# Attention logits of token tiles 4 to 7: two heads at a time in two column parts, with four logit buffers in place of two

## The chip, the cores and the metric

The kernel runs on one core of a Trainium2 chip. The metric is the device time of one execution in microseconds (us). Three runs of the kernel before gave 2792.24, 2794.49 and 2781.63 us, so the median is 2792.24 us.

The engines are PE (TensorE, matmuls), PEld (its weight loads, which overlap PE), DVE (VectorE), ACT (ScalarE), POOL (GpSimd) and SP (SyncE, which only issues DMAs here). Each engine runs its own instructions in order and waits for the others at semaphores.

## The reference

Two layers of a hybrid decoder over 1024 tokens of width 1024, all in float32. A layer projects the normed input once and gives it to three groups of heads (an mLSTM, a sparse attention, a Mamba-2 scan), joins their outputs by one projection, and ends with a SwiGLU feed-forward block. The change touches the sparse attention of four heads, each 64 wide:

```
score = where(causal, score, -inf)          # of a small indexer, shared by the heads
_, sel = lax.top_k(score, top_k)            # top_k = 256
logits = q . k_sel * (d ** -0.5)            # per head
p = softmax(logits)                         # over the selected keys that are causal
out = p @ v_sel
```

The kernel gathers nothing. It computes the logits of a query with all causal keys, adds a mask (0 for a selected key, a large negative number for another) and takes the softmax over the whole row. A tile of 128 queries number c (0 to 7) has 128(c+1) keys.

## The kernel before

Per layer there is a stage A (norm, the input projection in 30 units of 128 columns, the indexer, the choice of keys, the attention), a stage B (the scans, the output projection) and a stage E (feed-forward). A barrier over all engines stands between A and B of a layer. The E of layer 0 and the A of layer 1 share a block.

**A unit of the projection** is 48 matmuls over 512 columns (each weight and each activation is kept as a high and a low part, and three of the four products are taken), issued by `eighth(u, e)` in eighths of six, L891 to L901.

**The attention** is cut into 32 steps, step m = 4c + h for tile c and head h (`divmod(m, AH)`). A step goes through five places:

- PE, `two_logits(m)` (L1045 to L1051) for tiles 0 to 3, and `logits(m)` (L1030 to L1041) for tiles 4 to 7: the dot products of 128 queries with the tile's keys, over a contraction of 64. A head's 64 rows lie in the lower or the upper half of the partitions. `two_logits` issues both heads of a pair one behind the other at every even step, head i into its own PSUM bank (bank 2 or 3), over at most 512 columns. `logits` issues one head at every step, over 640 to 1024 columns, as one matmul of 512 columns and one of the rest, into banks 2 and 3 together (`pair23`).
- DVE, `maximum(m)` (L1278 to L1290): adds the mask, writes the sum into the logit buffer `lg[m % 2]` and reduces the row's maximum (L1286), then makes the bias of the exponential out of it (L1290).
- ACT, `exps(m)` (L742 to L747): the exponential in place, with its row sum.
- PE, `turn_weights(m)` (L1054 to L1060): c+1 transposes of 128x128 into banks 4 and 5, and ACT, `turned_out(m)` (L751 to L755), which copies them to `pt[m % 2]`.
- PE, `values(m)` (L1063 to L1071): c+1 matmuls with the values, 64 columns each.

DVE divides by the row sums in `rows_out(c)` (L1297, L1299), and PE turns the result in `cat_turn(c)` (L1078).

**The order on PE** is written out by hand. `attend(k)` (L1081) issues `values(k - 4)`, `turn_weights(k - 2)`, the logits of step k, and at every fourth k a `cat_turn`. Steps 0 to 7 stand in units 22 to 25, while DVE still searches for the selection threshold bit by bit. Steps 8 to 31 stand one behind each eighth of units 27, 28 and 29, and four calls behind the last unit empty the pipeline. I call one eighth with one `attend` a slot. DVE has `choose(c + 1, part)` (L1359 to L1371) behind each `attend` of tile c: it makes the mask of the next tile in four parts, of which part 1 is a scan (L1365). ACT has the evictions of the projection (L673) and `kept_hi` (L767) between its steps.

**The waits around the logits.** `logits(m)` waits for all maxima before m, since both heads share the two banks. `maximum(m)` waits for the transposes of step m - 2, which read the same buffer. `turn_weights(m)` waits for the exponential of m and for ACT's copy of step m - 1.

## Time and profile before

| what | value |
|---|---|
| median of 3 runs | 2792.24 us (2781.63 to 2794.49) |
| span of the profiled execution | 2787.1 us |
| PE busy | 2675.3 us, 96% of the span |
| PE weight loads busy | 2157.4 us, 77% |
| DVE busy | 1822.3 us, 65% |
| ACT busy | 1114.8 us, 40% |
| POOL busy | 1233.7 us, 44% |
| mean granted clock of TensorE, as a share of full speed | 0.981 |

The page gives the profiled execution by its span, from the first to the last instruction, and no time of its own beside it. The span is 5.1 us under the median of the runs. Busy PE is not PE at its peak, because matmuls overlap in the pipeline. What an instruction costs there is therefore read from start to start: the start of a group is taken from the start of the group behind it.

### The profile page before, as it was taken

Reading aid. Unit: us, or ns where it says so; the run is one execution under the profiler, and the core shown is the slowest. Engines: PE = TensorE matmul, PEld = TensorE weight load, DVE = VectorE, ACT = ScalarE, POOL = GpSimd, SP = SyncE. Lnnn points to the kernel's source line nnn. Section 1 sums busy time; section 2 is a strip of 40 time slices with the busy share of each in tenths; the row PEclk is TensorE's granted clock in tenths of the full one; section 3 lists DMA queues with packets and bytes.
Section 4 is the critical chain, followed back from the end, with each engine's and each line's share of the span. In section 5 each row is a group of like instructions: output and inputs, shape, how many; then the busy total and the mean of one; then the engine's idle time right before and its main releaser. Section 6 shows DMA issues by size and latency. Waiting matters only on the chain. (4 is left out here: it accounts for less than half of the span.)

```text
span 2787.1 us, 36014 instructions
## 1 busy us (share of the span) xinstructions
PE 2675.3 (96%) x12868; PEld 2157.4 (77%) x12868; DVE 1822.3 (65%) x2888; ACT 1114.8 (40%) x2094; POOL 1233.7 (44%) x774
## 2 busy tenths in 40 slices
PE   7999999999899999999989999999998999999997
PEld 5677877778688888888766788777786888888886
DVE  4469865584765666665654798646748566666666
ACT  4336434574532223232433364446745222323223
POOL 1228510340665545665433284104317544566545
PEclk9999999999999999999999999999999999999999
DMA  4102320433111111111421123105221211111113
GB/s 136 46 23 77 121 69 25 139 95 120 40 53 61 61 45 45 60 45 60 130 98 28 31 83 122 62 16 168 90 105 38 68 54 46 45 60 45 63 57 129
DMA packets 186882, 199.30 MB, mean 72 GB/s; under 512 B 19313, under 2 KB 162801, under 8 KB 186497
## 3 DMA queue, kind: packets, MB, share of 16 engines
q1 hardware_dynamic: 180992, 176.63, 20.3%
q10 hardware_dynamic: 5760, 20.97, 2.0%
q8 instruction: 78, 1.28, 0.2%
q14 instruction: 52, 0.42, 0.0%
HBM read 158.78 MB, written 38.80 MB: 71 GB/s over the span
## 5 line engine op out<-in xcount | busy, mean ns | idle before, releaser
L2271 POOL TENSOR_TENSOR ring_lo<-ring_sum,ring_hi 128x512 fp32r<-128x512 f32 x200 | 306.3, 1547 | 474.7 <-ACT ring_hi L2359 474.7
L2493 PE MATMUL ps<-form_hi,ring_hi 128*128 128x512 f32 x1232 | 484.2, 393 | 23.2 <-POOL ring_lo L1524 20.2
L2493 PE MATMUL ps<-form_lo,ring_hi 128*128 128x512 f32 x1232 | 482.5, 392 | 0.0
L2493 PE MATMUL ps<-form_hi,ring_lo 128*128 128x512 f32 x1232 | 482.3, 391 | 0.0
L901 PE MATMUL ps<-act_hi,whi 128*128 128x512 f32 x960 | 395.0, 411 | 9.2 <-ACT smr L441 8.4
L901 PE MATMUL ps<-act_lo,whi 128*128 128x512 f32 x960 | 379.0, 395 | 0.0
L901 PE MATMUL ps<-act_hi,wlo 128*128 128x512 f32 x960 | 378.7, 395 | 0.0
L2359 ACT ACTIVATE ring_hi<-ring_sum 128x512 fp32r<-128x512 f32 x200 | 125.2, 632 | 627.3 <-DVE ring_sum L2569 627.1
L2581 DVE TENSOR_TENSOR yacc<-yacc,ps 128x1024 f32<-128x1024 f32 x176 | 214.8, 1220 | 243.6 <-PE ps L2519 243.6
L1328 DVE TENSOR_SCALAR_CACHE_REDUCE ties<-score,kth 128x384 uint8<-128x384 f32 (+5 forms) x396 | 348.4, 942 | 4.8
L604 POOL TENSOR_TENSOR wlo<-raw,whi 128x1024 fp32r<-128x1024 f32 x56 | 137.2, 2449 | 394.0 <-ACT whi L646 394.0
L2493 PEld LDWEIGHTS ps<-form_hi,ring_hi 128*128 128x128 f32 x1232 | 233.5, 190 | 76.2 <-POOL ring_lo L1524 14.1
L2519 PE MATMUL ps<-ring_hi,hhi 128*128 128x512 f32 x704 | 275.3, 391 | 1.1 <-POOL hlo L2282 0.6
L2519 PE MATMUL ps<-ring_lo,hhi 128*128 128x512 f32 x704 | 274.4, 390 | 0.0
L2519 PE MATMUL ps<-ring_hi,hlo 128*128 128x512 f32 x704 | 274.3, 390 | 0.0
L2493 PEld LDWEIGHTS ps<-form_hi,ring_lo 128*128 128x128 f32 x1232 | 233.2, 189 | 48.8
L2493 PEld LDWEIGHTS ps<-form_lo,ring_hi 128*128 128x128 f32 x1232 | 233.4, 189 | 48.1
L901 PEld LDWEIGHTS ps<-act_hi,whi 128*128 128x128 f32 x960 | 183.0, 191 | 77.4 <-issue 35.9
L1570 DVE TENSOR_TENSOR gate_t<-gate_t,ps 128x512 f32<-128x512 f32 x176 | 116.9, 685 | 168.4 <-PE ps L2493 168.4
L901 PEld LDWEIGHTS ps<-act_hi,wlo 128*128 128x128 f32 x960 | 183.0, 191 | 40.2
L2569 DVE TENSOR_TENSOR ring_sum<-ff_raw 128x512 f32<-128x512 f32 x200 | 209.2, 1071 | 3.2 <-DMA ff_raw<-in_w_gate 3.2
L901 PEld LDWEIGHTS ps<-act_lo,whi 128*128 128x128 f32 x960 | 183.3, 191 | 36.1 <-issue 1.9
(321 smaller groups left out, 4686.9 us busy)
## 6 DMA issues: line engine op xcount, KB each, us to landing
raw<-in_w_in SPq DMA_DIRECT2D x56, 512.0 KB, 3.8
ff_raw<-in_w_gate SPq DMA_DIRECT2D x22, 1024.0 KB, 5.3
ff_raw<-in_w_up SPq DMA_DIRECT2D x22, 1024.0 KB, 5.3
ff_raw<-in_w_down SPq DMA_DIRECT2D x22, 1024.0 KB, 5.0
proj_scratch<-stage ACTq DMA_DIRECT2D x40, 512.0 KB, 2.7
wc<-proj_scratch SPq DMA_DIRECT2D x14, 1280.0 KB, 6.6
xmid_scratch<-xres SPq DMA_DIRECT2D x16, 512.0 KB, 2.6
resid<-xmid_scratch SPq DMA_DIRECT2D x16, 512.0 KB, 6.7
```

Of the source, the lines that this page charges most:

```text
L604: pool.tensor_tensor(wlo[u % 2][:, :], raw[u % 2][:, :], whi[u % 2][:, :].bitcast(F32), ALU.subtract)\
L901: mm = pe.matmul(ps[:, half, :], w[:, k], a[half][:, k, :], start=(k == 0 and m == 0), stop=(k == KT - 1 and m == 2))
L1328: v.tensor_scalar(tie(c), of(c), at(kth, c), 0.0, op, ALU.add, accum_out=at(held, c))
L1570: v.tensor_tensor(q, q, src, op).then_inc(m_drain.sem, 1)
L2271: pool.tensor_tensor(flat_form(ring_lo[slot]), src, flat_form(ring_hi[slot]).bitcast(F32), ALU.subtract)\
L2359: act.activation(flat_form(ring_hi[slot]), src, ACT.Copy).then_inc(f_hi.sem, 1)
L2493: mm = pe.matmul(ps[:, product_bank(r, i), :], w[:, k], a[:, k], start=(k == 0 and m == 0), stop=(k == 3 and m == 2))
L2519: mm = pe.matmul(place(t)[:, cols], h[:, j, rows], w, start=(j == 0 and m == 0), stop=(j == 1 and m == 2))
L2569: v.tensor_tensor(flat_form(ring_sum[slot]), weight_part(ff_raw[place[0]], *a), weight_part(ff_raw[place[0]], *b), op)\
L2581: v.tensor_tensor(yacc[t][:, :], yacc[t][:, :], place(t), ALU.add).then_inc(y_add.sem, 1)
```

## The change

1. `logits` is gone. `two_logits(m, part)` now serves all tiles. Tiles 4 to 7 go in two column parts, part 0 over the first 512 keys and part 1 over the rest (128, 256, 384 or 512). An even step issues part 0 of both heads, the odd step behind it part 1 of both. Head i of a pair goes into bank 2 + i.
2. On DVE, `maximum(m, part)` reduces one part of one head. The maxima have two places per head, and a new `bias(m)` takes the larger of both. An even step now does part 0 of both heads, an odd step part 1 and the bias of one head, then of the other.
3. There are four logit buffers. The two new ones are `nrow[0]` and `nrow[1]`, which hold norm weights in other stages. The maximum of m waits for the transposes of step m - 4.
4. In PE's `attend` the logits stand ahead of `turn_weights` and no longer behind it.

The core of the diff:

```diff
-            lg, pt, oatt = [iq[:, 0], iq[:, 1]], ...
-            mx, nb, sm_, rs = 32, 36, 40, 48
+            lg, pt, oatt = [iq[:, 0], iq[:, 1], nrow[0][:, :], nrow[1][:, :]], ...
+            clear, nb, sm_, rs, mx = 32, 36, 40, 48, 52
...
-            dots = lambda m: pair23 if m >= 4 * AH else ps[:, 2 + m % 2, :]
+            dots = lambda m: ps[:, 2 + m % 2, :]
+
+            def dots_before(m, part=0):
+
+                return m if m < ONE_PART else ONE_PART + 4 * ((m - ONE_PART) // 2) + 2 * part + m % 2
+
+            def part_of(c, part):
+
+                return slice(part * HALF, min((part + 1) * HALF, width[c]))
...
-                def logits(m):
...
-                        pe.wait_ge(*c_max(L, m if c >= 4 else m - 1))
-                    dst = dots(m)
-                    for b0 in range(0, width[c], HALF):
-                        b1 = min(b0 + HALF, width[c])
-                        mm = pe.matmul(dst[:, b0:b1], aq[q, h // 2, c * P:(c + 1) * P], ak[q, h // 2, b0:b1],
-                                       start=True, stop=True)
-                    mm.then_inc(c_qk.sem, 1)
-
-                def two_logits(m):
+                def two_logits(m, part):
...
-                    pe.wait_ge(*c_max(L, m))
+                    else:
+                        pe.wait_ge(*c_max(L, dots_before(m, part)))
+                    cols = part_of(c, part)
                     for i in range(2):
                         q = slice(HD * i, HD * i + HD)
-                        pe.matmul(dots(m + i)[:, 0:width[c]], aq[q, h // 2, c * P:(c + 1) * P], ak[q, h // 2, 0:width[c]],
+                        pe.matmul(dots(m + i)[:, 0:cols.stop - cols.start], aq[q, h // 2, c * P:(c + 1) * P], ak[q, h // 2, cols],
                                   start=True, stop=True).then_inc(c_qk.sem, 1)
...
                     if k >= 4:
                         values(k - 4)
+                    if k < N_PAIRS and k % 2 == 0:
+                        two_logits(k, 0)
+                    elif ONE_PART <= k < N_PAIRS:
+                        two_logits(k - 1, 1)
                     if 2 <= k < N_PAIRS + 2:
                         turn_weights(k - 2)
-                    if k < 4 * AH:
-                        if k % 2 == 0:
-                            two_logits(k)
-                    elif k < N_PAIRS:
-                        logits(k)
...
-                def maximum(m):
+                def maximum(m, part):
                     c, h = divmod(m, AH)
-                    if h == 0 and c >= 2:
+                    n = dots_before(m, part) + 1
+                    cols = part_of(c, part)
+                    if h == 0 and part == 0 and c >= 2:
                         v.wait_ge(*selected(L, c - 1))
-                    v.wait_ge(*c_qk(L, m + 1))
-                    if m >= 2:
-                        v.wait_ge(*c_turn(L, m - 1))
...
+                    v.wait_ge(*c_qk(L, n))
+                    if m >= 4 and part == 0:
+                        v.wait_ge(*c_turn(L, m - 3))
...
+                def bias(m):
+                    first, second, to = [small[:, k:k + 1] for k in (mx + m % 4, mx + 4 + m % 4, nb + m % 4)]
+                    if m < ONE_PART:
+                        v.wait_ge(*c_max(L, dots_before(m) + 1))
+                        v.tensor_scalar(to, first, -(HD ** -0.5), None, ALU.mult).then_inc(c_bias.sem, 1)
+                    else:
+                        v.wait_ge(*c_max(L, dots_before(m, 1) + 1))
+                        v.tensor_scalar(to, first, second, -(HD ** -0.5), ALU.max, ALU.mult).then_inc(c_bias.sem, 1)
...
-                    maximum(m)
+                    if m < ONE_PART:
+                        maximum(m, 0)
+                        bias(m)
+                    elif m % 2 == 0:
+                        maximum(m, 0)
+                        maximum(m + 1, 0)
+                    else:
+                        for i in (m - 1, m):
+                            maximum(i, 1)
+                            bias(i)
```

`ONE_PART` is 16, the first step of tile 4. `exps` and `turn_weights` take `lg[m % 4]` in place of `lg[m % 2]`.

**PE, two steps of tile 5** (heads 2 and 3; `avr` are the values, `ident` the unit matrix of a transpose, `ak`, `aq` the operands of the logits). Before:

```order
L1071 MATMUL ps<-avr,ik 128x64 [waits c_pt]
L1071 MATMUL ps<-avr,ik 128x64 x4
L1060 MATMUL ps<-ident,iq 128x128 [waits c_pt,c_exp]
L1060 MATMUL ps<-ident,iq 128x128 x5
L1041 MATMUL ps<-ak,aq 128x512 [waits c_max]
L1041 MATMUL ps<-ak,aq 128x256
```

and the two steps now, the even one and behind an eighth the odd one:

```order
L1071 MATMUL ps<-avr,ik 128x64 [waits c_pt]
L1071 MATMUL ps<-avr,ik 128x64 x4
L1051 MATMUL ps<-ak,aq 128x512 [waits c_max]
L1051 MATMUL ps<-ak,aq 128x512
L1060 MATMUL ps<-ident,iq 128x128 [waits c_pt,c_exp]
L1060 MATMUL ps<-ident,iq 128x128 x5
...
L1071 MATMUL ps<-avr,smw 128x64 [waits c_pt]
L1071 MATMUL ps<-avr,smw 128x64 x4
L1051 MATMUL ps<-ak,aq 128x256 [waits c_max]
L1051 MATMUL ps<-ak,aq 128x256
```

The two matmuls of a step, which were the two column parts of one head, are now one column part of both heads, and they stand ahead of the transposes.

**DVE, the two last steps of tile 4** (`lg` is `iq` or `nrow`; L1286 and then L1287 is the reduce, the 128x1 row behind it reads its result, L1290 and then L1298 is the bias, L1365 and L1367, then L1381 and L1383, are parts of `choose`). Before:

```order
L1285 MEMSET small 128x1 [waits c_turn,c_qk]
L1286 ISA iq,small<-ps,score 128x640
L1286 ISA small 128x1
L1290 TENSOR_SCALAR small<-small 128x1 [waits c_max]
L1367 SCALAR_TENSOR_TENSOR ties<-sinf,held,ties 128x768
L1285 MEMSET small 128x1 [waits c_turn,c_qk]
L1286 ISA iq,small<-ps,score 128x640
L1286 ISA small 128x1
L1290 TENSOR_SCALAR small<-small 128x1 [waits c_max]
```

and now:

```order
L1287 ISA nrow,small<-ps,score 128x512
L1287 ISA small 128x1
L1286 MEMSET small 128x1 [waits c_turn,c_qk]
L1287 ISA nrow,small<-ps,score 128x512
L1287 ISA small 128x1
L1383 SCALAR_TENSOR_TENSOR ties<-sinf,held,ties 128x768
L1286 MEMSET small 128x1 [waits c_qk]
L1287 ISA nrow,small<-ps,score 128x128
L1287 ISA small 128x1
L1298 TENSOR_SCALAR small<-small 128x1 [waits c_max]
L1286 MEMSET small 128x1 [waits c_qk]
L1287 ISA nrow,small<-ps,score 128x128
```

One reduce per head has become two, and both biases of a pair have moved into the odd step.

**PE, behind the last unit** (from step 31 on, now):

```order
L1051 MATMUL ps<-ak,aq 128x512 [waits c_max]
L1051 MATMUL ps<-ak,aq 128x512
L1060 MATMUL ps<-ident,iq 128x128 [waits c_pt,c_exp]
L1060 MATMUL ps<-ident,iq 128x128 x7
L1071 MATMUL ps<-avr,ik 128x64 [waits c_hi,c_pt]
L1071 MATMUL ps<-avr,ik 128x64 x7
L1060 MATMUL ps<-ident,nrow 128x128 [waits c_pt,c_exp]
L1060 MATMUL ps<-ident,nrow 128x128 x7
```

The transposes of step 29, which stood ahead of the last logits, stand behind them, and no eighth lies between the last logits and the transposes of step 30.

## Rows read from the trace of the kernel before

**Rows 1.** Stretches: length, busy (count) of PE, PEld, DVE, ACT, POOL; clock, DMA, GB/s.

```profile
422.00:441.00 19.00, 19.00 (x105) 14.20 (x105) 11.03 (x25) 9.04 (x17) 2.39 (x1) 1.00 0.19 63
...
501.00:511.00 10.00, 9.18 (x83) 8.94 (x82) 2.79 (x8) 5.88 (x12) 3.98 (x6) 1.00 0.17 66
...
1850.00:1861.00 11.00, 11.00 (x60) 7.95 (x59) 6.07 (x10) 4.59 (x8) 0.00 (x0) 1.00 0.01 1
```

**Rows 2.** Waits of PE by releaser, layer 0's attention: total, times, longest us.

```profile
PE ps L1738 <- POOL smem L1680: 2.1, 1, 2.1
PE ps L1078 <- DVE cosf L1299: 0.7, 1, 0.7
```

**Rows 3.** PE timeline (start, us): one head's logits, tiles 4 and 7.

```profile
422.65 1.34 PE L1041 MATMUL ps<-ak,aq 64*128 64x512 f32 x4
423.93 0.44 PE L1078 MATMUL ps<-ident,cosf 128*128 128x128 f32 x2
...
481.08 1.98 PE L1041 MATMUL ps<-ak,aq 64*128 64x512 f32 x4
482.99 0.44 PE L1078 MATMUL ps<-ident,cosf 128*128 128x128 f32 x2
```

**Rows 4.** PE timeline, layer 0: two heads' logits together, tiles 0 and 3, and what follows.

```profile
349.76 0.49 PE L1051 MATMUL ps<-ak,aq 64*128 64x128 f32 x4
350.18 0.50 PE L901 MATMUL ps<-act_hi,whi 128*128 128x512 f32 x1
...
410.08 1.13 PE L1051 MATMUL ps<-ak,aq 64*128 64x512 f32 x4
411.14 0.44 PE L1078 MATMUL ps<-ident,cosf 128*128 128x128 f32 x2
```

**Rows 5.** PE timeline, layer 0: what stands just ahead of a pair.

```profile
337.80 0.39 PE L901 MATMUL ps<-act_hi,wlo 128*128 128x512 f32 x1
338.12 0.49 PE L1051 MATMUL ps<-ak,aq 64*128 64x128 f32 x4
...
404.17 0.50 PE L1060 MATMUL ps<-ident,iq 128*128 128x128 f32 x3
404.59 0.92 PE L1051 MATMUL ps<-ak,aq 64*128 64x384 f32 x4
```

**Rows 6.** PE timeline: the tail of layer 0's attention.

```profile
500.73 2.00 PE L1071 MATMUL ps<-avr,ik 128*128 128x64 f32 x16
502.57 1.04 PE L1060 MATMUL ps<-ident,iq 128*128 128x128 f32 x8
503.45 0.38 PE L1078 MATMUL ps<-ident,cosf 128*128 128x128 f32 x2
```

**Rows 7.** DVE timeline: a reduce over 512 columns, and the long scan.

```profile
411.37 0.69 DVE L1286 CUSTOM_DVE_ANT_0 iq<-ps,score 128x512 f32<-128x512 f32 x1
...
468.01 2.29 DVE L1365 TENSOR_TENSOR_SCAN sinf<-ties 128x1024 f16<-128x1024 uint8 x1
```

**Rows 8.** ACT timeline: exponentials and what follows them.

```profile
412.29 0.72 ACT L747 ACTIVATE iq<-iq,small 128x512 f32<-128x512 f32 x1 [1.62 <-DVE small L1290]
...
502.30 1.15 ACT L747 ACTIVATE iq<-iq,small 128x1024 f32<-128x1024 f32 x1 [2.35 <-DVE small L1290]
...
503.45 0.58 ACT L673 ACTIVATE stage<-ps 128x512 f32<-128x512 f32 x1
...
504.49 1.02 ACT L755 ACTIVATE ik<-ps 128x1024 f32<-128x1024 f32 x1 [0.46 <-ACT stage L673]
```

**Rows 9.** PE timeline: the first chunk after the barrier, layer 0 and layer 1.

```profile
513.47 3.41 PE L1738 MATMUL ps<-ident,wc 128*128 128x128 f32 x14 [2.06 <-POOL smem L1680]
...
531.41 0.59 PE L1749 MATMUL ps<-unit_b,below 128*128 128x512 bf16 x2
...
1898.19 3.01 PE L1738 MATMUL ps<-ident,wc 128*128 128x128 f32 x14 [2.06 <-POOL smem L1680]
...
1911.62 0.59 PE L1749 MATMUL ps<-unit_b,below 128*128 128x512 bf16 x2
```

29 lines of the change are left out of this document (12 added, 17 removed).

## The prediction

> **What bounds the kernel now.** I read the busy table by stretches first, then PE's waits, then the PE timeline, and DVE and ACT last. In the dense stage of the attention (units 27 to 29 of the projection) PE is busy for the whole of every stretch, in layer 1 as in layer 0, at a granted clock of 1.00, which is the 2.4 GHz level, while DVE works 11.03 of 19.00 us and ACT 9.04 [rows 1]. From 330 to 515 us PE waits only twice: 0.7 us for the last `cat_turn`, and 2.1 us behind the barrier [rows 2]. So time that leaves PE's stream there leaves the layer, as long as nobody makes PE wait. The reader is to see that the attention's chain (logits, maximum, exponential, transposes) is spread over slots so widely that no latency shows: the steps cost PE's own time and nothing else.
>
> **What the logits cost, start to start.** One head of tile 4 (640 columns) takes 423.93 - 422.65 = 1.28 us, one of tile 7 (1024 columns) 482.99 - 481.08 = 1.91 us [rows 3]. That is 0.21 us per 128 columns, so tiles 5 and 6 take 1.49 and 1.70. Two heads issued together take 0.42 us over 128 columns and 1.06 us over 512 [rows 4], which is again 0.21 per 128 columns, so 0.63 over 256 and 0.85 over 384. The per-column price of a pair is that of one head: the two halves of the array work at the same time. The fixed part, 0.21, is paid by a group of either kind.
>
> **The sum on PE.** A pair of heads cost two singles, and now costs one part of 512 columns and one of the rest:
> - tile 4: 2 x 1.28 - 1.06 - 0.42 = 1.08 us
> - tile 5: 2 x 1.49 - 1.06 - 0.63 = 1.29 us
> - tile 6: 2 x 1.70 - 1.06 - 0.85 = 1.49 us
> - tile 7: 2 x 1.91 - 1.06 - 1.06 = 1.70 us
>
> Together 5.56, twice for the two pairs of a tile: 11.1 us per layer, 22.2 us for both.
>
> **The seams.** A group of logits now follows value matmuls, where it followed transposes. This seam is nowhere in the trace. The nearest rows: behind a projection matmul of 512 columns the pair starts after 0.32 us, where 512 columns at 2.4 GHz take 0.21, so 0.11 more [rows 5]. Behind three transposes it starts after 0.42, where eight transposes in a row take 0.88 and so three 0.33, thus 0.09 more [rows 5, 6]. I take the same 0.1 behind value matmuls, hence no change: there are 24 groups of logits per layer before (8 pairs, 16 singles) and 24 after (8 whole pairs, 16 parts). Bounds: a lead of 0 to 0.2, so 0.1 x 24 x 2 = 4.8 us either way. Ahead of transposes, as now always, a pair cost 1.06 with a transpose behind it [rows 4] and fits the same line as the ones with a projection matmul behind, so nothing is added there.
>
> **DVE.** Each head of tiles 4 to 7 gets a second reduce. From the start of a 512-column reduce to the exponential that needs it are 412.29 - 411.37 = 0.92 us, of which the reduce has 0.69 [rows 7, 8]; I take 1.0 per reduce with its bias. An odd step of tile 6 then takes DVE 2.0 us, and the scan behind it up to 2.29 [rows 7], 4.3 in all from the end of the odd logits. PE has the transposes (7 x 0.11), an eighth (6 x 0.21 = 1.3), twelve value matmuls at 1.84/16 each (1.4) and the next part 0 (0.1 + 1.06) until DVE's next operand exists: 4.6 us. DVE is free 0.3 us earlier, and even if it were not, PE asks for those maxima only one slot later. The cover is thin only on DVE's own side; I cost it at nothing. If it went, PE would wait at part 1 of the next pair.
>
> **ACT and the transposes.** The exponential of an even step m now starts only when its part 1 is reduced, about 1.1 us after the odd logits end. It takes up to 1.15 (502.30 to 503.45), and the copy of step m - 1 behind it 1.02 [rows 8]: 3.3 us. PE gets to the transposes of m after those of m - 1 (0.88), an eighth (1.3), fourteen values (1.6) and a pair (1.16), that is 4.9 us. Hidden, with 1.6 us to spare.
>
> **The tail** is the one place where this cover is missing. Behind the last logits (end T) PE has only the transposes of step 29 (0.88) and the values of step 28 (1.84) [rows 6], so it wants the transposes of step 30 at T + 2.7; ACT's copy is done at about T + 3.3, and a semaphore later it is T + 3.4. The wait is 0.7 us per layer, 1.4 for both. After it the copies of steps 30 and 31 come just in time by the same rows. Bounds: 0 to 1.5 us per layer. The transfer of the last unit keeps its place: its eviction follows the last exponential as before, and both move together, some 8 us ahead of the barrier.
>
> **What is late next.** Nothing before the barrier overlaps with B, so what A loses, the layer loses. Behind the barrier PE waits 2.06 us for POOL's clearing of `smem` [rows 9], before and after. Steps 0 to 7 keep their waits: the logits move ahead of one transpose, and DVE needs them one of its long counting rounds later.
>
> **Sum:** -22.2 + 1.4 = -20.8 us. The durations are those of the profiled execution, span 2787.1 us, so its span would be 2766.3. Against the median of the runs, 2792.24, it is 2771.4 us, 0.74% less. A measurement of this kernel can tell about 0.5%, 14 us, from no change, so the border of faster is 2778.3.
>
> **The clock** is the largest thing that isn't in the sum. In layer 0 the first chunk of B ran from 513.47 to 531.41, 17.9 us, and in layer 1 the same work from 1898.19 to 1911.62, 13.4 us [rows 9]. After the idle time at the barrier the granted clock stood at the lower level, 1.2 GHz, for longer in layer 0. This is 4.5 us that either layer can have or not have, whatever the change does; it goes into the range, not into the value.
>
> **The rivals.**
> - *Stalls take back half.* Each of the 16 pairs of both layers makes PE wait 0.5 to 0.8 us, because the biases of a pair now come together in the odd step, where before they came one per slot. Against it stands the spare of 1.6 us above. For it: both exponentials of a pair follow each other on ACT, with a copy between, and an eviction of a projection half (0.58 [rows 8]) falls in as well. It gives 8 to 13 us back: 2779 to 2784.
> - *The two parts don't overlap* as in tiles 0 to 3, for example because a second column part of the same rows has to wait for the first. Then a pair costs its columns twice, and the time stays at 2792 +- 5. The pairs of tiles 0 to 3 speak against it [rows 4]: same shapes, same banks, same instruction.
> - *DVE becomes the bound, and the kernel slower.* Place: two slots of tile 6 and 7, where DVE has four reduces, two biases, a scan and another part of `choose`. Four reduces over 2 x (512 + 384) columns move 2.5 us of data, biases, `rows_out` and `choose` take about 4.2, and each reduce has a fixed part x. Before, two such slots took PE 10.7 us (2 x (1.70 + 1.3 + 1.4 + 0.9)). DVE decides if 4x + 6.7 is over 10.7, that is from x = 1.0 on. At x = 1.2, DVE would need 11.5, and 0.8 us more in each of 16 pairs make +13: 2805. The rows give x as 0.92 - 0.69 = 0.23, a bias included [rows 7, 8], and DVE idles 40% of the stage, which speaks against it.
>
> The Trainium skill speaks for this last rival: "TensorEngine Tiling (Array Packing)", section Performance Considerations, says that packing speeds up the matmuls and not the reading of PSUM, which may become the bottleneck. By that rule alone the gain would be capped by DVE's load, and no run here shows it yet; the trace, with DVE busy for 11.03 of 19.00 us while every tile's logits pass through it [rows 1], does not agree.
>
> **How the numbers follow.** The forecast as summed has 0.74, with its own range 2763 to 2779 (seams 4.8, clock 4.5, the tail). Stalls that take back half have 0.15. No overlap has 0.04, DVE as the bound 0.04, and 0.03 are left for something slower or faster that I don't see. The forecast lies on the near side of 2778.3 but for a small part, and the gentlest of the stall cases with it: faster 0.77. The rest of the stalls, no overlap and the forecast's upper end make no change, 0.18; slower has 0.05. The range of 8 in 10 goes from 2762 up to 2781, which takes in the milder stalls.
>
> **What would show it.** In the timeline of the changed kernel a part 0 costs 1.06 us start to start and the parts 1 cost 0.42, 0.63, 0.85 and 1.06. PE's waits between 330 us and the barrier show nothing of over 0.1 us in the dense stage, and one of about 0.7 at the transposes of step 30, released by ACT's copy (L755's successor). The barrier of layer 0, after 511.86 us before, comes some 10.4 us earlier. DVE's busy time grows by about 2 x 16 x 0.25 = 8 us. I am wrong if a part 0 takes over 1.3 us, if PE's waits in the dense stage add up to over 4 us per layer, or if the stage shortens as said and the whole does not.

## The result and the profile after

The changed kernel takes 2761.19 us (median of 4 runs, 2760.58 to 2761.63); the kernel before 2787.03 (4 runs, 2781.63 to 2794.49: two of them at 2781.7, two over 2792). The ratio is 0.989 (95% interval 0.9873 to 0.9907): faster by 1.1%. The gain was 25.8 us where 20.8 were forecast, and the time lies 0.8 us below the low end of the range. The profiled executions differ by 27.4 us of span.

The page of the changed kernel: span and busy time by engine.

```profile
span 2759.7 us, 36108 instructions
...
PE 2650.1 (96%) x12868; PEld 2148.3 (78%) x12868; DVE 1825.1 (66%) x2984; ACT 1110.2 (40%) x2094; POOL 1231.8 (45%) x774
```

PE has the same 12868 matmuls as before, and 25.2 us less busy time. DVE has 96 instructions more and 2.8 us more. So the change took time out of PE's own stream, and it was not bought with waits: these are PE's waits of the changed kernel from 330 to 505 us, in the form of [rows 2].

```profile
PE ps L1754 <- POOL smem L1696: 2.1, 1, 2.1
PE ps L1078 <- DVE cosf L1306: 0.7, 1, 0.7
PE ps L1060 <- ACT smw L765: 0.6, 1, 0.6
```

Two are those of before. The third is new: the tail wait, forecast at 0.7 us. In the dense stage nothing stands. The PE timeline shows the prices of the parts; each is the start of the next row less that of its own.

```profile
422.01 1.13 PE L1051 MATMUL ps<-ak,aq 64*128 64x512 f32 x4
423.07 0.66 PE L1060 MATMUL ps<-ident,nrow 128*128 128x128 f32 x4
...
426.10 0.49 PE L1051 MATMUL ps<-ak,aq 64*128 64x128 f32 x4
426.52 0.66 PE L1060 MATMUL ps<-ident,nrow 128*128 128x128 f32 x4
...
441.28 0.70 PE L1051 MATMUL ps<-ak,aq 64*128 64x256 f32 x4
441.91 0.77 PE L1060 MATMUL ps<-ident,nrow 128*128 128x128 f32 x5
...
458.21 0.92 PE L1051 MATMUL ps<-ak,aq 64*128 64x384 f32 x4
459.06 0.87 PE L1060 MATMUL ps<-ident,nrow 128*128 128x128 f32 x6
```

1.06, 0.42, 0.63 and 0.85 us, for two heads each time: to the hundredth the prices that tiles 0 to 3 had before, of which [rows 4] shows 0.42 and 1.06. From the last logits on, part 1 of tile 7 at 1.06 us, the timeline reads:

```profile
486.75 1.13 PE L1051 MATMUL ps<-ak,aq 64*128 64x512 f32 x4
487.81 1.09 PE L1060 MATMUL ps<-ident,iq 128*128 128x128 f32 x8
488.74 1.90 PE L1071 MATMUL ps<-avr,ik 128*128 128x64 f32 x16
491.19 1.06 PE L1060 MATMUL ps<-ident,nrow 128*128 128x128 f32 x8 [0.56 <-ACT smw L765]
...
492.31 1.90 PE L1071 MATMUL ps<-avr,smw 128*128 128x64 f32 x16
494.29 1.06 PE L1060 MATMUL ps<-ident,nrow 128*128 128x128 f32 x8
...
499.60 0.44 PE L1078 MATMUL ps<-ident,cosf 128*128 128x128 f32 x2 [0.73 <-DVE cosf L1306]
502.10 2.93 PE L1754 MATMUL ps<-ident,wc 128*128 128x128 f32 x14 [2.06 <-POOL smem L1696]
...
515.54 0.59 PE L1765 MATMUL ps<-unit_b,below 128*128 128x512 bf16 x2
```

The first matmul behind the barrier starts at 502.10, where it was 513.47 [rows 9]: 11.4 us earlier, forecast 10.4. The last row is the start of the second chunk of B: the first chunk took 515.54 - 502.10 = 13.4 us, and before 17.9 [rows 9]. That is another 4.5 us, and it has nothing to do with the logits. The stretches (columns as in [rows 1]) show what it has to do with; first three of the changed kernel, then three of the kernel before.

```profile
422.00:441.00 19.00, 19.00 (x121) 14.94 (x120) 12.27 (x42) 7.92 (x16) 2.39 (x1) 1.00 0.19 63
502.00:508.00 6.00, 5.41 (x47) 3.74 (x49) 0.00 (x0) 2.81 (x6) 2.65 (x4) 0.72 1.06 280
1902.00:1920.00 18.00, 17.79 (x96) 15.79 (x97) 11.24 (x27) 10.03 (x31) 4.49 (x5) 0.53 0.36 103
```

```profile
512.00:528.00 16.00, 14.06 (x77) 11.12 (x78) 3.91 (x9) 7.64 (x19) 5.67 (x10) 0.57 1.00 279
1898.00:1904.00 6.00, 5.33 (x45) 3.69 (x47) 0.00 (x0) 2.81 (x6) 2.75 (x4) 0.72 1.00 266
1932.00:1938.00 6.00, 5.89 (x38) 5.73 (x39) 4.91 (x14) 2.45 (x7) 1.61 (x2) 0.72 0.39 113
```

In the dense stage PE holds 121 matmuls where it held 105 in the same 19 us, the clock is 1.00, and DVE has 12.27 us of work, not 11.03 [rows 1]. Behind the barrier of layer 0 the granted clock is at the 1.2 GHz level for a good part of 6 us in the changed kernel, and for nearly all of 16 us in the one before. In layer 1 it is the other way round: the changed kernel has 18 us at mostly 1.2 GHz (0.53) some 30 us behind its barrier, the one before only bits of the two stretches shown and a third from 1994 to 2001 us.

**Where the 27.4 us are.** I took the attention from the first value matmul of step 4 to the last `cat_turn` (398.54 to 510.97 before, 398.48 to 499.60 after), and counted every start-to-start time on PE to the kind of matmul that it begins with:

| us, layer 0 | logits | values | transposes | cat_turn | projection | whole |
|---|---|---|---|---|---|---|
| before | 29.28 | 30.97 | 16.59 | 1.38 | 34.21 | 112.42 |
| after | 18.22 | 33.45 | 14.67 | 1.04 | 33.74 | 101.12 |
| difference | -11.06 | +2.48 | -1.92 | -0.34 | -0.46 | -11.30 |

The logits gave 11.06, forecast 11.1. The +2.48 of the values holds the tail wait, 0.56. What is left, 1.92 - 1.92 - 0.34 - 0.46 = -0.80, is the seams. Counted from the first value matmul of all, at step 0, to the last `cat_turn` the attention went from 149.57 us to 138.18, the same to 0.01 us in both layers: 11.39 less in each, 22.8 in both. The other 4.6 us of the spans lie where the change has no instruction. B, counted from the end of the last `cat_turn` to the end of the output projection, went from 199.2 to 193.9 us in layer 0 and from 196.1 to 198.8 in layer 1, together 2.6 less; the stretch from there to layer 1's attention took 2.1 less. The granted clock stood at its lower level for 27.4 us of the two Bs before and for 27.3 after: the sum is the same, and what differs is where it fell.

### The profile page after: what moved, and what is told of

Read it like the earlier page. It is cut to its first block and busy times, and to the rows that moved or that the text cites. A ratio compares the mean times of both kernels' runs of the same rounds, so it can differ in the third digit from the quotient of the medians.

```text
span 2759.7 us, 36108 instructions
## 1 busy us (share of the span) xinstructions
PE 2650.1 (96%) x12868; PEld 2148.3 (78%) x12868; DVE 1825.1 (66%) x2984; ACT 1110.2 (40%) x2094; POOL 1231.8 (45%) x774
## 3 DMA queue, kind: packets, MB, share of 16 engines
q1 hardware_dynamic: 180992, 176.63, 20.5%
## 5 line engine op out<-in xcount | busy, mean ns | idle before, releaser
L2509 PE MATMUL ps<-form_hi,ring_hi 128*128 128x512 f32 x1232 | 484.2, 393 | 22.8 <-POOL ring_lo L1540 19.7
L911 PEld LDWEIGHTS ps<-act_hi,whi 128*128 128x128 f32 x960 | 183.0, 191 | 64.1 <-issue 23.8
```

The source lines that it names most:

```text
L911: mm = pe.matmul(ps[:, half, :], w[:, k], a[half][:, k, :], start=(k == 0 and m == 0), stop=(k == KT - 1 and m == 2))
L2509: mm = pe.matmul(ps[:, product_bank(r, i), :], w[:, k], a[:, k], start=(k == 0 and m == 0), stop=(k == 3 and m == 2))
```

## Experiments

The questions were: is the gain the overlap of the two halves, or the new order and the two more buffers; how thin is DVE's cover; what removes the tail wait; and where the rest comes from, the clock above all. A second copy of either kernel ran beside the experiments. The attention is counted from the first value matmul to the last `cat_turn`; layer 0 is shown, and layer 1 is within 0.01 us of it in all but dve_double. The kernels ran in four groups, each on a chip of its own and beside further runs of the kernel before: the first four of the table, the next four, the last four, and the shifts at the end.

| kernel | attention, us | median us (runs) | lowest to highest | ratio to before (95%) |
|---|---|---|---|---|
| before_again | 149.57 | 2792.73 (10) | 2781.27 to 2795.45 | 1.0 |
| order_only | 148.30 | 2780.89 (10) | 2777.26 to 2785.61 | 0.9971 (0.9958 to 0.9983) |
| split_pairs | 154.39 | 2797.02 (10) | 2791.61 to 2801.60 | 1.0019 (1.0007 to 1.0031) |
| eighth_last | 137.17 | 2762.27 (4) | 2754.19 to 2764.80 | 0.9895 (0.9867 to 0.9923) |
| after_again | 138.18 | 2758.79 (4) | 2757.92 to 2759.38 | 0.9891 (0.9874 to 0.9907) |
| before_fill | 149.56 | 2782.55 (10) | 2781.47 to 2783.54 | 0.9977 (0.9965 to 0.9990) |
| after_fill | 138.18 | 2758.73 (4) | 2757.99 to 2761.31 | 0.9893 (0.9876 to 0.9909) |
| order_fill | 148.30 | 2778.69 (7) | 2775.00 to 2782.65 | 0.9954 (0.9939 to 0.9969) |
| after_third | 138.18 | 2757.67 (5) | 2755.49 to 2764.84 | 0.9873 (0.9852 to 0.9894) |
| dve_half | 138.32 | 2759.98 (2) | 2759.50 to 2760.46 | 0.9884 (0.9853 to 0.9915) |
| dve_double | 139.12 | 2765.70 (2) | 2763.08 to 2768.33 | 0.9905 (0.9872 to 0.9937) |
| last_fill | 137.18 | 2756.97 (5) | 2756.31 to 2757.84 | 0.9874 (0.9853 to 0.9895) |

The kernel before had medians of 2791.35, 2790.96, 2795.01 and 2791.52 us beside the four groups, and all its 83 runs in this study lie between 2780.93 and 2796.68, with a median of 2791.6. That is a spread of 16 us in a kernel that nobody touched; the changed kernel's 13 runs lie between 2755.49 and 2764.84, median 2758.8.

### Order and buffers alone, the overlap, and the tail

**before_again** is the kernel before, unchanged.

> The kernel before, unchanged, profiled once more. Theory (the gain of the change is the 20.8 us of PE work less the tail's wait, and what came on top, some 5 us of the median, is where the granted clock happened to stand at the lower level): the four runs of the kernel before so far lie at 2781.6, 2781.8, 2792.2 and 2794.5 us; a new profile differs from the first by several us of span, every bit of it in stretches at 1.2 GHz behind an idle PE (512 to 528 us above all), while layer 0's attention, from the values of step 4 to the last turn of the output, takes 112.4 +- 0.2 us again. Rival (the extra gain is the change's own): the new profile's span is within 1 us of 2787 and its stretches at the lower level are the same ones.

It settled that the spread belongs to the kernel and not to one set of runs. The attention is the same again; the span is 6.5 us longer than in the first profile, and all of it lies in the two Bs (1.2 and 5.3 us).

**order_only** is the kernel before with four logit buffers and the logits ahead of the transposes; tiles 4 to 7 stay one head at a time.

```diff
-            lg = [iq[:, 0], iq[:, 1]]
+            lg = [iq[:, 0], iq[:, 1], nrow[0][:, :], nrow[1][:, :]]
...
-                    if m >= 2:
-                        v.wait_ge(*c_turn(L, m - 1))
+                    if m >= 4:
+                        v.wait_ge(*c_turn(L, m - 3))
...
-                    if 2 <= k < N_PAIRS + 2:
-                        turn_weights(k - 2)
                     if k < 4 * AH:
...
                         logits(k)
+                    if 2 <= k < N_PAIRS + 2:
+                        turn_weights(k - 2)
```

> The kernel before with four logit buffers and the logits ahead of the transposes, but one head at a time as before. Theory: pairing brings 11.1 us a layer, the new order only the seams, which I read as 0.8 us a layer from the two profiles (values +1.9, transposes -1.9, what stood behind logits -0.8), less a wait of about 0.6 at the tail. So layer 0's attention takes 112.0 to 112.6 us against 112.4, and the whole is within 3 us of the kernel before at the same clock. Rival (the earlier logits and the free buffers take latency out of the chain): the attention gets over 3 us shorter per layer.

The attention fell by 1.27 us per layer, 1.18 of them from step 4 on, to 111.24, where the theory had 112.0 to 112.6: logits 29.29 (+0.01), values 32.48 (+1.52), transposes 14.63 (-1.96), cat 1.04 (-0.34), projection 33.80 (-0.41). So the seams are a gain of the new order with its buffers, the whole of the -0.80 and more, and none of the logits' 11.06 is. It has no tail wait. Its median, though, is 10.5 us under that of the kernel before, 8 more than its two attentions give; the clock section comes back to this. Two steps of its PE timeline:

```profile
421.97 1.00 PE L1071 MATMUL ps<-avr,ik 128*128 128x64 f32 x8
422.90 1.34 PE L1041 MATMUL ps<-ak,aq 64*128 64x512 f32 x4
424.17 0.66 PE L1060 MATMUL ps<-ident,nrow 128*128 128x128 f32 x4
...
428.47 0.66 PE L1060 MATMUL ps<-ident,nrow 128*128 128x128 f32 x4
428.88 0.48 PE L901 MATMUL ps<-act_hi,whi 128*128 128x512 f32 x1
```

Eight values now cost 0.93 (they cost 0.84 with transposes behind), the logits 1.27 as before, and four transposes 0.41 with a projection matmul behind. A change of kind costs PE something at either side of the logits; it is the sum over all the seams that moved, and none of these by more than 0.12 us.

**split_pairs** is the changed kernel with the two heads of each part kept apart on PE: the transposes stand between them. DVE's parts, the buffers and the number of matmuls stay.

```diff
+                    split = ONE_PART <= k < N_PAIRS
                     if k < N_PAIRS and k % 2 == 0:
-                        two_logits(k, 0)
+                        two_logits(k, 0, (0,) if split else (0, 1))
-                    elif ONE_PART <= k < N_PAIRS:
-                        two_logits(k - 1, 1)
+                    elif split:
+                        two_logits(k - 1, 1, (0,))
                     if 2 <= k < N_PAIRS + 2:
                         turn_weights(k - 2)
+                    if split:
+                        two_logits(k - k % 2, k % 2, (1,))
```

> The changed kernel, but in tiles 4 to 7 the transposes stand between the matmuls of head 0 and those of head 1, so that the two heads can't run at the same time; same instructions, same DVE and ACT work. Theory (the gain is the overlap of two heads in the two halves of the array): every part is paid twice, 2 x (1.06 + 0.42, 0.63, 0.85, 1.06) per pair, which is 14.4 us more per layer, and 16 more seams of 0.1: layer 0's attention goes from 101.1 to 115.5 to 117.1 us, the whole to 2790 to 2793, above the kernel before. Rival (order, buffers, DVE's smaller pieces): the attention stays under 106 us.

```profile
422.33 1.12 PE L1051 MATMUL ps<-ak,aq 64*128 64x512 f32 x2
423.38 0.66 PE L1060 MATMUL ps<-ident,nrow 128*128 128x128 f32 x4
423.97 1.12 PE L1051 MATMUL ps<-ak,aq 64*128 64x512 f32 x2
425.02 0.44 PE L1078 MATMUL ps<-ident,cosf 128*128 128x128 f32 x2
```

One head's 512 columns cost 1.05 us, the second head's 1.05 again, and both together 1.06. So the second head is free when it follows the first at once, and costs its full price when something stands between. The attention grew to 154.39 us, 16.2 more than with the pairs, 14.2 of it in the logits (14.4 expected). It is 4.8 more than before: 3.1 because 16 more groups of logits pay their fixed part, and 1.7 at the seams. From step 4 on it is 117.3 us, where 115.5 to 117.1 were expected, and the median, 2797.02, is 4 us above its range. This is the gain, shown.

**eighth_last** puts the last eighth of the last unit behind the last logits and transposes, where it covers the tail.

```diff
                     for e in range(8):
-                        eighth(u, e)
+                        last = u == N_PROJ - 1 and e == 7
+                        if not last:
+                            eighth(u, e)
                         attend(EARLY + 8 * (u - U_LATE) + e)
+                        if last:
+                            eighth(u, e)
```

> The changed kernel with the last eighth of the last projection unit behind the last logits instead of ahead of them, as a cover at the tail. Theory (PE waits 0.56 us there because exponential and copy of 3.3 us meet only 2.7 us of PE work): with 1.4 us more work in between the wait is gone, each layer is 0.6 us shorter, the whole 1.1 us, unless the later spill of the last unit, which has some 8 us to spare, shows at the barrier. Rival: the wait is a semaphore's latency and stays, or the wait moves to the next transposes: no change within 0.3 us.

```profile
484.80 1.89 PE L1071 MATMUL ps<-avr,ik 128*128 128x64 f32 x16
486.53 1.04 PE L1060 MATMUL ps<-ident,nrow 128*128 128x128 f32 x8
...
487.63 1.90 PE L1071 MATMUL ps<-avr,smw 128*128 128x64 f32 x16
489.36 1.04 PE L1060 MATMUL ps<-ident,nrow 128*128 128x128 f32 x8
```

The transposes of step 30 follow the values without a wait, and the attention is 1.01 us shorter per layer. Start to start these values take 1.73 us where they took 491.19 - 488.74 = 2.45 in the changed kernel, so the tail wait is worth 0.72 and not only its 0.56 of idle time. The values behind them take 1.73 where they took 1.98, there and in the kernel before: 0.25 more. order_only has 1.73 in that place too, so 0.25 of its 1.18 are this and 0.93 are seams; with the tail at 0.72 the changed kernel's seams are 0.96, the same within 0.03. In the medians the edit does not show (2762.27, runs over 10 us apart). last_fill below comes back to it.

### How much room DVE has

Both kernels add a dummy pass of DVE over the logits in PSUM ahead of the reduce, whose result nobody reads: dve_half ahead of part 0 only, dve_double ahead of both parts. after_third is the changed kernel once more.

```diff
+                    if m >= ONE_PART:
+                        v.drain()
+                        v.tensor_tensor(cosf[:, HALF:HALF + cols.stop - cols.start], dots(m)[:, 0:cols.stop - cols.start],
+                                        score[:, sbase[c] + cols.start:sbase[c] + cols.stop], ALU.add)
                     v.tensor_tensor_reduce(lg[m % 4][:, cols], dots(m)[:, 0:cols.stop - cols.start],
```

> The changed kernel a third time, for the spread of its runs: 8 so far lie at 2757.9 to 2761.6 us, where 60 of the kernel before lie at 2781 to 2796. Theory A (it lands in the scans at another place of the same slow wander of the clock, and can lose as much): some of the new runs are over 2764 us. Theory B (the change keeps it out of the low clock in stage B): all are within 2756 to 2763.

> The changed kernel with a useless DVE addition of the same 512 columns (0.69 us, and a drain of DVE ahead of it) before each reduce of a part 0 of tiles 4 to 7, its result never read. From the profile of the changed kernel DVE is busy for 9.94 of 14.85, 11.11 of 16.59, 12.31 of 18.36 and 5.71 of 16.89 us of tiles 4 to 7. The additions make it 13.1, 14.3, 15.5 and 8.9. Theory (DVE is covered with room): no wait of PE in the dense stage over 0.3 us, layer 0's attention 101 to 101.6 us. Rival (DVE is nearly the bound, as the rule on the reading of PSUM has it): the attention grows by 2 us or more.

> The same before every reduce of tiles 4 to 7, both parts. DVE's load becomes about 14.6 of 14.85, 16.3 of 16.59, 18.1 of 18.36 and 12.0 of 16.89 us. Theory: here the room ends; with nothing left for latency PE starts to wait at the logits (for the maxima) or at the transposes (for the exponential), 1 to 2 us per tile of 4 to 6 and 1 us more at the tail, so the attention takes 104 to 108 us. Rival (PE's slots, with two steps of lookahead, swallow even that): under 102.5 us. If it is over 110 us, DVE was much nearer to the bound than its busy time tells.

Two stretches of dve_double's dense stage, and the wait at its tail:

```profile
437.00:453.50 16.50, 16.50 (x108) 13.05 (x107) 15.18 (x43) 7.28 (x15) 0.00 (x0) 1.00 0.01 1
453.50:472.00 18.50, 18.50 (x122) 14.57 (x121) 16.84 (x44) 8.14 (x15) 0.00 (x0) 1.00 0.07 30
```

```profile
PE ps L1060 <- ACT smw L765: 1.3, 1, 1.3
```

DVE works 15.18 of 16.50 and 16.84 of 18.50 us, and PE is still busy for the whole of both stretches. In the dense stages of both layers PE waited 0.5 us for DVE in all, both times in layer 1, and the tail wait grew from 0.6 to 1.3. So layer 0 lost 0.94 us, and at half the load (dve_half) 0.14: from step 4 on dve_double's layer 0 takes 102.1 us, so the rival's "under 102.5" holds there and the theory's 104 to 108 does not. DVE is not the bound at this load, but its waits are not free. In layer 1 of dve_double's profiled execution the granted clock fell right behind the tail wait, to a mean of 0.81 from 1856 to 1874 us, ahead of the barrier; the next values took 3.30 us where they take 1.98, and the attention took 142.79 us, 4.6 more than without the load. From step 4 on that is 105.7 us, inside the theory's range, but most of it by the clock and not by waits. The two medians differ from after_third by 2.3 and 8.0 us, with two runs each.

after_third has one run over 2764 us (2764.84), as its Theory A has it: the changed kernel is not kept out of the low clock.

The change itself put less on DVE than one would add up. By form, one reduce of the kernel before, and the pieces now:

```profile
L1286 DVE CUSTOM_DVE_ANT_0 iq<-ps,score 128x1024 f32<-128x1024 f32 x4 | 4.9, 1222 | 13.4 <-issue 13.4
L1286 DVE CUSTOM_DVE_ANT_0 iq<-ps,score 128x640 f32<-128x640 f32 x4 | 3.3, 821 | 5.6 <-issue 5.6
```

```profile
L1287 DVE CUSTOM_DVE_ANT_0 nrow<-ps,score 128x512 f32<-128x512 f32 x12 | 8.0, 686 | 11.2 <-issue 11.2
L1287 DVE CUSTOM_DVE_ANT_0 nrow<-ps,score 128x128 f32<-128x128 f32 x4 | 1.2, 288 | 0.9 <-issue 0.9
```

2 x 0.686 - 1.222 = 0.15 us for tile 7, and 0.686 + 0.288 - 0.821 = 0.15 for tile 4. The rows are of layer 0.

### The clock

The theory after the first four kernels: PE's many short idle times in B (waits of 0.4 to 2.3 us for POOL, ACT and DVE) let the granted clock fall to 1.2 GHz in some executions and not in others, and this is both the spread and the part of the gain that the attention does not account for. The **fill** kernels put transposes of the unit matrix where PE waits: 12 behind the last `cat_turn`, 8 at the start of B, and 18 in each of two waits of the first chunks, 56 per layer, into PSUM columns that are written anew before anyone reads them. Their results are used nowhere. before_fill, order_fill and after_fill have the same lines.

```diff
                 cat_turn(NT - 1)
+                pe.wait_ge(*evicted(N_PROJ - 1))
+                for _ in range(12):
+                    pe.transpose(ps[:, 0, 0:P], ident[:, :], ident[:, :])
...
             def b_tensor(pe):
+                for _ in range(8):
+                    pe.transpose(bank(7)[:, 0:P], ident[:, :], ident[:, :])
...
+                    if c in (1, 2):
+                        for _ in range(18):
+                            pe.transpose(bank(b)[:, 0:P], ident[:, :], ident[:, :])
                     pe.wait_ge(*m_out(L, c + 1))
```

> The changed kernel once more. Layer 0's and layer 1's attention (first values of step 4 to the last turn of the output) take 101.1 us each again. Theory A (what the whole gained beyond the attention, some 5 to 8 us, is only where the lower clock happens to fall): more runs spread over 8 us or more, as those of the kernel before do (2781 to 2796), and their median comes to within 3 us of 2791.35 - 22.6 = 2768.8. Theory B (the change shifts stage B against something fixed, so that the lower clock falls there less): the runs stay at 2760 to 2765.

> The kernel before with idle transposes of the unit matrix where PE otherwise stands idle around the barrier (12 behind the last turn of the attention, 8 ahead of the first wait of B) and ahead of two waits of 2.3 us in the scan loop (18 each). Their result is never read. They show what the low clock in stage B costs. If the idle time is what lets the clock fall there, the stretches at 1.2 GHz between 510 and 580 us and at 1898 to 1954 are gone, the runs lie closer together (within 4 us), and the whole is 2779 to 2785 us although PE does more. If other gaps or the kind of work let it fall, the stretches stay and the time grows by 1 to 5 us.

> The changed kernel with the same idle transposes. Theory (extra gain = clock in B): against the kernel before with the same filling the difference is the attention's, 22.6 +- 1.5 us, and not the 25 to 30 that the two kernels show without it. Rival (the change wins elsewhere too): the difference stays at 25 to 30 us.

> The order-only kernel (one head at a time, logits ahead of the transposes, four buffers) with the same idle transposes. Its attention is 1.2 us per layer shorter than that of the kernel before, its whole was 10.5 us shorter. Theory: with the filling the whole is 2.4 +- 1.5 us shorter than the filled kernel before. Rival: it stays some 8 to 10 us shorter, and then the early order does something outside the attention.

Stretches of before_again, then of before_fill, over the same parts of B (layer 0, then layer 1):

```profile
512.00:516.00 4.00, 2.96 (x14) 2.53 (x14) 0.00 (x0) 2.48 (x3) 1.12 (x5) 0.57 0.68 200
560.00:578.00 18.00, 17.41 (x94) 15.42 (x95) 11.62 (x27) 11.18 (x33) 4.27 (x6) 0.53 0.35 103
1898.00:1912.00 14.00, 12.11 (x64) 9.26 (x65) 3.01 (x7) 6.55 (x17) 3.73 (x8) 0.51 0.98 276
1938.00:1954.00 16.00, 16.00 (x96) 13.95 (x96) 10.59 (x26) 9.58 (x30) 4.26 (x5) 0.57 0.40 116
```

```profile
510.00:526.00 16.00, 14.12 (x126) 12.22 (x127) 6.49 (x18) 8.69 (x22) 8.06 (x13) 1.00 0.86 243
536.00:578.00 42.00, 39.81 (x354) 33.48 (x356) 38.81 (x80) 30.82 (x96) 20.32 (x19) 1.00 0.53 156
1898.00:1904.00 6.00, 6.00 (x52) 5.61 (x50) 4.01 (x10) 4.19 (x14) 3.24 (x4) 1.00 1.16 316
1932.00:1954.00 22.00, 20.25 (x178) 16.91 (x173) 19.82 (x41) 17.89 (x56) 9.11 (x8) 1.00 0.48 141
```

Without the fill PE's granted clock is at or near 0.53 for tens of microseconds of B; with it, at 1.00 throughout. The kernel with more work in it is the faster one: 2782.55 against 2790.96, its ten runs lie within 2.1 us where the unfilled kernel's lie within 16, and they lie at the fast edge of those. Over the whole span PE spent 123.9 us at 1.2 GHz in before_again and 76.9 in before_fill; the 76.9 lie outside the Bs. Work done at half the clock takes twice its time, so 47.0 us less of it are worth up to 23.5 us; the spans differ by 12.8, and 112 transposes at 0.11 us [rows 6] are up to 12.3 us added. The Trainium skill has the same rule in "TensorE: Matmul & The Clock Gate", section Terms: the penalty is about the time at the reduced clock times the share of pulses left out; these two runs fit it but do not test it closely, since the gain is 12.8 us with none of the added work counted and 25.1 with all of it.

What a B costs in each profiled execution shows the same more directly. The table gives its length, from the end of the last `cat_turn` to the end of the output projection, and in brackets how long the granted clock stood at 1.2 GHz in it. B is the same program in all the rows without a fill.

| us | B of layer 0 | B of layer 1 |
|---|---|---|
| before | 199.2 (13.7) | 196.1 (13.7) |
| before_again | 200.3 (20.5) | 201.4 (27.3) |
| order_only | 194.8 (10.2) | 194.0 (6.8) |
| after | 193.9 (6.8) | 198.8 (20.5) |
| after_again | 194.0 (6.8) | 194.7 (10.2) |
| before_fill, order_fill, after_fill | 194.4 to 194.5 (0) | 194.4 to 194.5 (0) |

With the clock held in B, the comparison is cleaner: before_fill less after_fill is 23.8 us, of which the two attentions are 22.8; before_fill less order_fill is 3.9, and the attentions are 2.5, where without the fill the difference was 10.5. The fill does not hold everything: order_fill's seven runs still lie 7.7 us apart, and 27 to 44 us at 1.2 GHz lie between the B of layer 0 and the attention of layer 1, with or without it. In the changed kernel the same fill gained nothing (2758.73 against 2758.79): it stood at the favourable end without it. after_again fits neither of its theories: four runs within 1.5 us, and a median under the 2760 to 2765 of Theory B.

**last_fill** is after_fill with the edit of eighth_last.

> The changed kernel with both the last eighth behind the last logits and the idle transposes around the barrier and in two waits of the scans. Each layer's attention takes 100.1 us, as with the moved eighth alone, against 101.1; the stretches at 1.2 GHz in stage B are gone as in the filled kernels. Theory: 2 us under the changed kernel with the filling (2758.7), so 2756.7 +- 1, with runs within 3 us of each other. Rival: the two don't add up, 2758 to 2761.

2756.97 against after_fill's 2758.73: 1.8 us less, where two attentions shorter by 1.0 each make 2.0. Its five runs lie within 1.5 us. Layer 1's B still has 2.9 us at 1.2 GHz in its profile, where the other filled kernels have none. The two ran on different chips, and the kernel before differs by 4 us in its medians there, so the 1.8 fit the attentions but do not prove them; the attentions themselves are in the traces (137.18 and 138.18). It has the lowest median of the study, 0.7 us under that of after_third on the same chip, which is within after_third's spread.

**The shifts.** Two theories remained for why the changed kernel's median was nearly free of the clock's loss and that of the kernel before not. N: the new attention ends differently, and leaves PE in a better state for B. P: only the moment at which B's short idle times come matters, and the changed attention happened to move B to a good one. Each kernel got 16 (s1) or 32 (s2) dummy transposes in each layer ahead of unit 27, far from both barriers, which move all behind them by about 1.7 or 3.4 us per layer.

```diff
                     project(u)
+                pe.wait_ge(*evicted(U_LATE - 1, 0))
+                for _ in range(16):
+                    pe.transpose(ps[:, 0, 0:P], ident[:, :], ident[:, :])
                 for u in range(U_LATE, N_PROJ):
```

> The kernel before with 16 idle transposes ahead of unit 27 in each layer: 1.7 us more work per layer and everything behind them later by that, nothing else changed. Theory P (the loss of 8 us in stage B is a matter of where B's short idle times fall in time, and a shift changes it): the median differs from 2791.35 + 3.4 = 2794.8 by over 3 us, downward if the usual place of this kernel is a bad one. Theory N (the kernel before loses more because of how its attention ends): the median is 2793 to 2797.

> The same with 32 transposes, 3.4 us per layer. Theory P: again off 2791.35 + 6.8 = 2798.2 by some us, and not by the same amount as with 16. Theory N: 2796 to 2800.

> The changed kernel with 16 idle transposes ahead of unit 27 in each layer. Its median over 13 runs is 2759. Theory P: off 2762.4 by over 2 us, upward if its own place is a good one. Theory N: 2761 to 2764.

> The same with 32 transposes. Theory P: off 2765.8 by over 2 us. Theory N: 2764 to 2768. Over both pairs: if P holds, the difference between the kernel before and the changed one at the same shift lies anywhere between 20 and 33 us and not always at 30; if N holds it is 29 to 33 at each.

| | median us (runs) | with the added transposes alone | difference |
|---|---|---|---|
| before | 2791.52 (19) | | |
| before_s1 | 2789.58 (10) | 2794.8 | -5.2 |
| before_s2 | 2799.37 (10) | 2798.2 | +1.2 |
| after_s1 | 2768.15 (4) | 2762.4 | +5.7 |
| after_s2 | 2765.12 (4) | 2765.8 | -0.7 |

The third column is that of the expectations. In the traces 16 transposes lengthen the two attentions by 3.5 us and 32 by 7.0, counted from 2791.52 and, for the changed kernel, from 2758.8; that moves no difference by more than 0.4. The changed kernel did not run unshifted on this chip, and its shifted versions have four runs each. The profiled execution of after_s1 has two long stretches at the lower level in layer 0 where the changed kernel had two short ones (6.8 us in all). They are shown first, then the same parts of B in before_s1:

```profile
504.00:518.00 14.00, 12.71 (x68) 9.85 (x69) 3.16 (x6) 6.58 (x18) 4.23 (x8) 0.51 1.03 290
544.00:560.00 16.00, 16.00 (x94) 13.90 (x94) 10.56 (x26) 9.83 (x30) 4.41 (x6) 0.57 0.40 116
```

```profile
512.00:520.00 8.00, 5.13 (x23) 3.31 (x26) 0.70 (x2) 3.73 (x6) 3.68 (x8) 0.57 0.63 170
548.00:554.00 6.00, 4.71 (x28) 4.67 (x29) 5.32 (x12) 3.09 (x8) 2.48 (x3) 0.72 0.18 51
```

The changed attention did not protect its B: moved by 1.7 us, the kernel loses 5.7 in its median, and layer 0's B takes 201.5 us in the trace, 27.3 of them at 1.2 GHz. The kernel before, moved by the same, gains 5.2 in its median; that is only just clear of noise, since the interval of before_s1 against the kernel before is 0.9986 to 1.0013, 3.9 us under to 3.6 over it, with 3.5 over it expected. The gap between the two kernels is 21.4 us under the first shift and 34.3 under the second, outside N's 29 to 33 both times, and the second also outside P's 20 to 33. N falls. P is not confirmed as it was put: under the second shift both kernels came out within 1.2 us of the added work, inside N's ranges and not where P has them. What is shown is that a shift alone can put a B into the low clock for long.

The traces show more of P than the medians do. In the profiled executions without a fill, 14 of them with two Bs each, the granted clock falls at the same places of B every time: once around the waits of 0.7 us ahead of the barrier and 2.1 us behind it, and once at the scans' wait of 2.3 us for DVE; two Bs have a third fall behind a wait of 1.3 us. Only the time at 1.2 GHz differs. At the scans' wait it goes with when the fall comes. In 20 of the 28 Bs it came 0.2 to 1.5 us behind the end of the wait, and lasted 3.4 us. In four it came 1.6 to 1.8 us behind it and lasted 13.7, and in four at its end or up to 0.3 us ahead of it, and lasted 17.1. So a good moment and a bad one are tenths of a microsecond apart. What sets this moment in an execution stays open: before and before_again differ by 5.3 us in layer 1's B with nothing edited, and order_only enters layer 0's B within 0.4 us of where they do and takes 194.8 us for it where they take 199.2 and 200.3.

## Why the prediction was right or wrong

- **What the logits cost.** Right to 0.1 us per layer: 11.06 measured, 11.1 forecast, each part at its price, and split_pairs shows that it is the overlap.
- **The seams** were taken as nothing, with bounds of 4.8 us either way. They gave 0.90 us per layer, 0.80 of them from step 4 on, 1.8 in all, well inside. The step that was too short: I compared the number of logit groups and what precedes each, where both neighbours of the transposes change too. order_only shows that they come from the new order and its buffers (-1.27 per layer, 0.25 of it a wait that is gone).
- **DVE and ACT hidden.** Right. PE has no wait in the dense stage. DVE's busy time was put at +8 us and grew by 2.8. The rows of the reduce and the bias together grew by 4.3, from 60.1 to 64.4 us: a split costs 0.15 in the move itself, and what comes with it mostly overlaps with it. The rest of DVE's busy time differs by 4 us between two profiles of the changed kernel.
- **The tail.** 0.56 us of idle time per layer, 0.72 from start to start, 0.7 forecast; mechanism, place and releaser as said, and eighth_last removes it.
- **The barrier** came 11.4 us earlier, 10.4 forecast: the seams' 0.90 and the tail's 0.14.
- **No overlap, stalls that take back half:** neither occurred, by the prices and by the empty list of waits.
- **DVE as the bound:** ruled out with room in the changed kernel. "TensorEngine Tiling (Array Packing)", section Performance Considerations, in the Trainium skill warns that reading PSUM may become the bottleneck once matmuls are packed; with DVE at 15.18 of 16.50 us, dve_double shows PE still without a gap in that stretch; at that load layer 1 had 0.5 us of waits for DVE. The two slots of PE that the rival adds up make 10.6 us and not 10.7; nothing hangs on it.
- **The step that failed** is "it goes into the range, not into the value". The clock was named as the largest thing outside the sum and given 4.5 us either way, from one pair of first chunks [rows 9]. That was too small, and taken from one place. Low stretches come in the scans too, not only in the first chunk: in the profiled executions one B took from 193.9 to 201.5 us, up to 27.3 of them at 1.2 GHz, so 7.6 us for each layer in place of 4.5. Nor was it centred: with B held at full clock the kernel before is 8.4 us faster in its median although it does more (before_fill), so a change that moves its B had more to win than to lose. That last step is argued and not shown. Nothing in the prediction said which way the clock's share would go, so where the forecast is concerned its sign is luck.
- **The sum of the miss.** Against 2771.4 the time is 10.2 us lower. The attentions gave 22.8 where 20.8 were forecast: 2.0, of them 1.8 of seams, 0.3 of the tail and -0.1 of the logits. The profiled executions differ by another 4.6 with nothing of the diff in it, 2.6 of them in the two Bs and 2.1 between these (rounded). Some 3.3 are the step from the span to the median: the forecast added 5.1 to the span, where every later execution takes 1.9 or less over its own, so the profiled one took about 2789 (my estimate from these) and lay 3.3 under the median of the three runs. The last 0.4 lie between the profiled execution and the median of the changed kernel. Without these 4.6 the time would have lain inside the range.
- **The size of the gain** depends on which runs of the kernel before it is held against. By the four runs it is 25.8, by the medians of 83 and 13 runs 32.8, with B's clock held 23.8. Only the attention's 22.8 belong to the change.

## What to carry to other kernels

- Two matmuls with 64 rows each on different halves of the array cost as one if nothing stands between them on PE. If a reader cannot hold both results, split the columns before you give up the pair; the price is one more reduce each, here 0.15 us on an engine with room.
- Cost each group start to start, from the same shape elsewhere in the kernel. The logits' sum held to 0.1 us per layer. And count both sides of every seam that a new order makes.
- Where a kernel has a stage with many short idle times on PE, look at its granted clock by stretches in several executions before you trust a difference of a few microseconds. Fill the idle times of both kernels and compare those: the spread of the kernel before fell from 16 us to 2, and its difference to order_only from 10.5 us to 3.9, where the attentions say 2.5. And read the stage that you changed, and the ones that you did not, by themselves: the attention repeats to 0.01 us where the whole moves by 16.

## What the runs showed of the hardware

- The same B, with nothing changed in it, took from 193.9 to 201.5 us in the profiled executions. A shift of 1.7 us moved the median of the changed kernel up by 5.7; one of 3.4 us moved it by no more than the added work.
- One head's 512 columns take 1.05 us, and those of two heads issued one behind the other 1.06.
